# Gated recurrence of a two-block layer on one core: decay sums as pairs of fp32r matmuls, masks one step sooner, three heads' norms together

## What is computed

```python
def gla_scan(k, v, log_a, s0, q):            # 4 heads, dk 128, dv 256, two directions
    # per chunk of 64 positions
    bcum = jnp.cumsum(ac, axis=2)
    b_end = bcum[:, :, -1, :]
    k_to_end = kc * jnp.exp(b_end[:, :, None, :] - bcum)
    s_new = jnp.exp(b_end)[..., None] * s + einsum('bhik,bhiv->bhkv', k_to_end, vc)
    rel = jnp.where(tril, bcum[:, :, :, None, :] - bcum[:, :, None, :, :], -inf)
    scores = einsum('bhjk,bhik,bhjik->bhji', qc, kc, jnp.exp(rel))
    o = einsum('bhji,bhiv->bhjv', scores, vc) + einsum('bhjk,bhkv->bhjv', qc * jnp.exp(bcum), s)

gla_loga = log_sigmoid(dec) / 16             # the decays
y_gla = rmsnorm(gla_o, gla_g_norm) * silu(gla_gate)      # per head, over 256 values
```

## Time and profile before

| | us |
|---|---|
| median of 3 runs | 2233.95 |
| lowest, highest | 2231.99, 2235.13 |
| profiled execution | 2231.3 |
| its span, first to last instruction | 2229.6 |

### The profile page before, as it was taken

One profiled execution on the slowest core, in us unless ns is written; L12 is line 12 of the kernel. 1 busy time (PEld: TensorE's weight loads), 2 busy tenths in 40 slices (PEclk: granted clock), 3 DMA queues, 4 the chain that ended last, 5 costly groups with the idle time before them and its releaser, 6 DMA issues.

```text
span 2229.6 us, 29088 instructions
## 1 busy us (share of the span) xinstructions
PE 2168.6 (97%) x10083; PEld 1742.8 (78%) x10083; DVE 1494.2 (67%) x2235; ACT 1055.2 (47%) x1317; POOL 50.6 (2%) x99
## 2 busy tenths in 40 slices
PE   7999999999999999999999999989999999999998
PEld 6777778878787777877788777768888888888886
DVE  6456657867675888775665677567777777875554
ACT  5344435644444444545433544445555555554443
POOL 0000000000001000000000001000000000000000
PEclk9999999999999999999999999999999999999999
DMA  8877778977777979875444335555655555567664
GB/s 311 280 262 248 270 237 292 325 240 268 243 273 233 316 236 347 305 259 157 132 124 135 104 95 189 173 168 173 199 178 188 180 184 191 179 196 229 193 192 144
DMA packets 279637, 482.03 MB, mean 216 GB/s; under 512 B 21726, under 2 KB 112960, under 8 KB 277744
## 3 DMA queue, kind: packets, MB, share of 16 engines
q1 hardware_dynamic: 274544, 464.93, 63.2%
q0 software_dynamic: 4992, 15.76, 2.1%
HBM read 474.15 MB, written 6.46 MB: 216 GB/s over the span
## 4 chain that ended last, share of the span: by engine, by line
PE 86%; DVE 6%; issue 3%; ACT 3%; DMA 2%; SPq 0%; DVEq 0%; ACTq 0%
PE gemm_ps L1764 74%; DVE w_lo L1035 2%; DMA w_raw<-in_w_in_dram 2%; ACT w_hi L617 1%; PE ps L1808 1%; PE ps L2167 1%; PE ps L2210 1%; DVE tmpT L1067 1%; PE ps L2314 1%; DVE msum L1202 1%; PE ps L2233 1%; DMA w_raw<-in_w_out_dram 1%; PE ps L1847 1%; PE ps L1817 0%; PE ps L1856 0%
## 5 line engine op out<-in xcount | busy, mean ns | idle before, releaser
L1035 DVE TENSOR_TENSOR w_lo<-w_raw,w_hi 128x1024 fp32r<-128x1024 f32 (+1 forms) x688 | 826.9, 1214 | 510.6 <-ACT w_hi L617 504.5
L1764 PE MATMUL gemm_ps<-w_hi,a_hi 128*128 128x512 f32 (+1 forms) x2304 | 920.0, 399 | 26.3 <-DVE w_lo L1035 13.4
L617 ACT ACTIVATE w_hi<-w_raw 128x1024 fp32r<-128x1024 f32 (+1 forms) x688 | 709.7, 1050 | 461.4 <-PE gemm_ps L1764 319.5
L1764 PE MATMUL gemm_ps<-w_hi,a_lo 128*128 128x512 f32 (+1 forms) x2304 | 899.2, 390 | 0.0
L1764 PE MATMUL gemm_ps<-w_lo,a_hi 128*128 128x512 f32 (+1 forms) x2304 | 898.2, 390 | 0.0
L1764 PEld LDWEIGHTS gemm_ps<-w_hi,a_hi 128*128 128x128 f32 x2304 | 435.4, 189 | 144.3 <-issue 29.6
L1764 PEld LDWEIGHTS gemm_ps<-w_hi,a_lo 128*128 128x128 f32 x2304 | 435.1, 189 | 92.7
L1764 PEld LDWEIGHTS gemm_ps<-w_lo,a_hi 128*128 128x128 f32 x2304 | 436.1, 189 | 85.5 <-issue 1.0
L1668 DVE SCALAR_TENSOR_TENSOR acc<-gp,cw,acc 128x256 f32<-128x256 f32 x344 | 151.4, 480 | 13.8 <-DVE acc L1668 1.4
L1202 DVE SCALAR_TENSOR_TENSOR msum<-mraw,cs,msum 128x1024 f32<-128x1024 f32 x120 | 153.0, 1275 | 0.7
L1764 PE MATMUL gemm_ps<-w_hi,ft_hi 128*128 128x512 f32 x344 | 135.0, 392 | 2.2 <-DVE w_lo L1035 2.2
(11 more groups left out here) (402 smaller groups left out, 1448.6 us busy)
## 6 DMA issues: line engine op xcount, KB each, us to landing
w_raw<-in_w_in_dram SPq DMA_DIRECT2D x336, 512.0 KB, 4.6
mraw<-in_w_mod_dram SPq DMA_DIRECT2D x192, 512.0 KB, 6.2
w_raw<-in_w_up_dram SPq DMA_DIRECT2D x336, 256.0 KB, 3.0
w_raw<-in_w_down_dram SPq DMA_DIRECT2D x84, 512.0 KB, 4.3
w_raw<-in_w_out_dram SPq DMA_DIRECT2D x64, 512.0 KB, 4.7
w_raw<-in_w_up_dram SPq DMA_DIRECT2D x24, 512.0 KB, 5.2
x_d<-xres POOLq DMA_DIRECT2D x2, 2048.0 KB, 8.0
x_sb<-in_x_dram SPq DMA_DIRECT2D x2, 1024.0 KB, 5.9
```

Of the source, the lines that this page charges most:

```text
L617: act.activation(w_hi[:, slot, :, 0:n], raw[:, slot, :, 0:n], ACT.Copy).then_inc(hi_done, 1)
L1035: dve.tensor_tensor(w_lo[:, slot, :, 0:n], raw[:, slot, :, 0:n], w_hi[:, slot, :, 0:n].bitcast(F32), ALU.subtract).then_inc(lo_done, 1)
L1764: mm = pe.matmul(gemm_ps[:, bank, rt, 0:n], x[:, chunk0 + k, rt * P:(rt + 1) * P], w[:, slot, kk, 0:n], start=(k == 0 and part == 0), stop ...
```

## The change

It does four things.
1. Each sum of decays, before one float32 matmul, becomes two fp32r matmuls that accumulate in the same bank: one with `la_hi`, the decays' high part, and one with `la_lo`, the rest. ScalarE makes `la_hi` per head (`decays_hi`, at v = 1 of the head before), VectorE makes `la_lo` in place (`decays_lo`, steps 63, 67, 73, 79). `lsum` becomes fp32r: it is loaded raw, without waiting for the state, and ScalarE copies it at step 62; the edge constants are copied in place at step 34. TensorE waits for `la_split` at v = 1.
2. On VectorE `gla_mask` moves from step 65 + k to step 64 + k, and stands behind `gla_mult` of the step.
3. The norms of heads 0 to 2 are taken together at step 91; that of head 3 stays at 96.
4. The buffers `masked` move.

```diff
--- before.py
+++ after.py
@@ -306,7 +306,9 @@
     gates = at("gates", [P, RT, D], F32, 153.5)
     state = at("state", [P, 2, HEADS, GDV], F32, 129.5)
     gqT = at("gqT", [P, 2, 2, T], F32, 137.5)
-    lsum = at("lsum", [P, 2, sum(GROUP_COLS)], F32, 141.5)
+    lsum_raw = at("lsum_raw", [P, 2, sum(GROUP_COLS)], F32, 97.5)
+    lsum = at("lsum", [P, 2, sum(GROUP_COLS)], F32R, 141.5)
+    edge_sums = at("edge_sums", [P, 4 * P], F32R, 80 + CONST_AT["suf_ex"][0] * 4 / KB)
     lexp = at("lexp", [P, 2, LEVELS - 1, 2, HALF], F32, 97.5)
     lq = at("lq", [P, LEVELS - 1, P], F32, 104.5)
     lk = at("lk", [P, LEVELS - 1, P], F32, 108)
@@ -314,7 +316,9 @@
     hsq = at("hsq", [P, RT, GDV], F32, 187.5)
     mden = at("mden", [P, T], F32, 187.5)
     lpair = at("lpair", [P, LEVELS, P], BF16, 149.5)
-    masked = [at("masked0", [P, 4, P], F32, 185.5), at("masked1", [P, 4, P], F32, 201.5)]
+    masked = [at("masked0", [P, 4, P], F32, 93.5), at("masked1", [P, 4, P], F32, 95.5)]
+    la_hi = [at("la_hi0", [P, RT, 2, HD], F32R, 185.5), at("la_hi1", [P, RT, 2, HD], F32R, 201.5)]
+    la_lo = at("la_lo", [P, RT, 2, NBLK], F32R, 189.5)
     sc = at("sc", [P, 4, P], F32, 111.5)
     gtb = at("gtb", [P, D], F32, 129.5)
     gtr = at("gtr", [2, D], F32, 137.5)
@@ -566,8 +570,9 @@
             pool.dma_start(x1_d, xres[:]).then_inc(S("x1_out"), 16)
             sum_store(5, SUMS)
 
+            pool.dma_start(lsum_raw[:], a["lsum"].rearrange("p (d c) -> p d c", d=2)).then_inc(S("lsum_in"), 16)
+            pool.wait_ge(S("lsum_in"), 16)
             pool.wait_ge(S("g_state"), 2)
-            pool.dma_start(lsum[:], a["lsum"].rearrange("p (d c) -> p d c", d=2)).then_inc(S("lsum_in"), 16)
             pool.dma_start(lpair[:], a["lpair"].rearrange("p (l t) -> p l t", l=LEVELS)).then_inc(S("lsum_in"), 16)
             pool.wait_ge(S("y_ready"), 2 * HEADS)
             pool.wait_ge(S("x1_out"), 16)
@@ -841,6 +846,8 @@
                     if m >= 2:
                         act.wait_ge(S("g_kend"), m - 1)
                     act.activation(kexp[m % 2][:, :], (pC, pA)[m % 2], ACT.Exp).then_inc(S("g_kexp"), 1)
+                if s == 34:
+                    act.activation(edge_sums[:, :], C("suf_ex", n=4 * P), ACT.Copy)
                 if 34 <= s < 62:
                     h, i = (s - 34) // 7, (s - 34) % 7 + 2
                     if i == 2:
@@ -856,6 +863,11 @@
                     act.wait_ge(S("g_S"), 1)
                     act.activation(state[:, 0].rearrange("p h v -> p (h v)"), ps[:, 0:2].rearrange("p a b -> p (a b)"),
                                    ACT.Copy).then_inc(S("g_state"), 1)
+                    act.wait_ge(S("g_la"), 8)
+                    act.wait_ge(S("lsum_in"), 16)
+                    for d in range(2):
+                        act.activation(lsum[:, d], lsum_raw[:, d], ACT.Copy)
+                    decays_hi(0)
                 if 64 <= s <= 64 + 6 * HEADS:
                     gla_consume(s - 64)
                 if 66 <= s < 70:
@@ -885,6 +897,12 @@
                 act.wait_ge(S("g_ps"), turn[0] + 1)
                 turn[0] += 1
                 return ps[:, (turn[0] - 1) % 2]
+
+            def decays_hi(h):
+
+                if h:
+                    act.wait_ge(S("la_split"), 2 * h)
+                act.activation(la_hi[h % 2][:], la[:, :, :, h * HD:(h + 1) * HD], ACT.Copy).then_inc(S("la_split"), 1)
 
             def gla_consume(k):
 
@@ -910,6 +928,10 @@
                             act.wait_ge(S("g_mult"), last_use)
                         src = bank[:, 0:GROUP_COLS[g]].rearrange("p (c l s) -> p c l s", c=2, s=HALF)
                         act.activation(lexp[:, :, lo:hi, 1 - d, :], src, ACT.Exp).then_inc(S("g_free"), 1)
+                if v == 1 and h + 1 < HEADS:
+                    if h:
+                        act.wait_ge(S("g_ps"), TURNS(6 * h - 1))
+                    decays_hi(h + 1)
                 if v == 4:
                     for rt in range(RT):
                         bank = take()
@@ -1525,9 +1547,14 @@
                 if s == 62:
                     dve.wait_ge(S("g_S"), 1)
                     dve.tensor_copy(state[:, 1].rearrange("p h v -> p (h v)"), ps[:, 2:4].rearrange("p a b -> p (a b)")).then_inc(S("g_state"), 1)
-                if 65 <= s < 65 + 6 * HEADS + 2:
-                    gla_mask(s - 65)
-                    gla_mult(s - 65)
+                if s == 63:
+                    decays_lo(0)
+                if 67 <= s < 67 + 6 * (HEADS - 1) and (s - 67) % 6 == 0:
+                    decays_lo((s - 67) // 6 + 1)
+                if 64 <= s < 65 + 6 * HEADS + 1:
+                    if s > 64:
+                        gla_mult(s - 65)
+                    gla_mask(s - 64)
                 if s == 72:
                     dve.wait_ge(S("y_ss_m"), HEADS)
                     head_norms(slice(HEADS, 2 * HEADS))
@@ -1535,10 +1562,12 @@
                     if s == 84:
                         dve.wait_ge(evac_act, 40)
                     gated(HEADS + s - 84)
-                if 78 <= s < 78 + 6 * HEADS and (s - 78) % 6 == 0:
-                    h = (s - 78) // 6
-                    dve.wait_ge(S("y_ss"), h + 1)
-                    head_norms(slice(h, h + 1))
+                if s == 91:
+                    dve.wait_ge(S("y_ss"), HEADS - 1)
+                    head_norms(slice(0, HEADS - 1))
+                if s == 96:
+                    dve.wait_ge(S("y_ss"), HEADS)
+                    head_norms(slice(HEADS - 1, HEADS))
                 if s in (92, 93, 98, 99):
                     h = (92, 93, 98, 99).index(s)
                     dve.wait_ge(evac_act, 41 + h // 2)
@@ -1558,6 +1587,11 @@
 
 
             tiles = (((0, 0, T), (1, 0, T), (2, 0, T), (3, P, T)), ((0, 0, T), (1, 0, T), (3, 0, T), (2, 0, P)))
+
+            def decays_lo(h):
+                dve.wait_ge(S("la_split"), 2 * h + 1)
+                own = slice(h * HD, (h + 1) * HD)
+                dve.tensor_tensor(la_lo[:, :, :, own], la[:, :, :, own], la_hi[h % 2][:].bitcast(F32), ALU.subtract).then_inc(S("la_split"), 1)
 
             def gla_mult(k):
 
@@ -2184,7 +2218,11 @@
             def gla_fill(k):
 
                 h, v = k // 6, k % 6
-                L = lambda t, d: la[:, t, d, h * HD:(h + 1) * HD]
+                def sums(out, t, d, of):
+
+                    pe.matmul(out, la_hi[h % 2][:, t, d], of, start=True, stop=False)
+                    return pe.matmul(out, la_lo[:, t, d, h * HD:(h + 1) * HD], of, start=False, stop=True)
+
                 if v == 0 and h < HEADS:
                     if h == 0:
                         pe.wait_ge(S("g_state"), 2)
@@ -2203,19 +2241,18 @@
                     return
                 if v in LEVEL_FILLS:
                     rt, g = LEVEL_FILLS[v]
-                    if k == 1:
-                        pe.wait_ge(S("lsum_in"), 32)
+                    if v == 1:
+                        pe.wait_ge(S("la_split"), 2 * (h + 1))
                     at_col = sum(GROUP_COLS[:g])
                     for d in range(2):
-                        pe.matmul(give()[:, 0:GROUP_COLS[g]], L(rt, d), lsum[:, d, at_col:at_col + GROUP_COLS[g]],
-                                  start=True, stop=True).then_inc(S("g_ps"), 1)
+                        sums(give()[:, 0:GROUP_COLS[g]], rt, d, lsum[:, d, at_col:at_col + GROUP_COLS[g]]).then_inc(S("g_ps"), 1)
                 if v == 4:
                     bank = give()
-                    pe.matmul(bank[:, 0:2 * P], L(0, 0), C("suf_ex", n=2 * P), start=True, stop=True)
-                    pe.matmul(bank[:, 2 * P:3 * P], L(0, 1), C("suf_in"), start=True, stop=True).then_inc(S("g_ps"), 1)
+                    sums(bank[:, 0:2 * P], 0, 0, edge_sums[:, 0:2 * P])
+                    sums(bank[:, 2 * P:3 * P], 0, 1, edge_sums[:, 3 * P:]).then_inc(S("g_ps"), 1)
                     bank = give()
-                    pe.matmul(bank[:, 0:P], L(1, 0), C("pre_in"), start=True, stop=True)
-                    pe.matmul(bank[:, P:3 * P], L(1, 1), C("pre_ex", n=2 * P), start=True, stop=True).then_inc(S("g_ps"), 1)
+                    sums(bank[:, 0:P], 1, 0, edge_sums[:, P:2 * P])
+                    sums(bank[:, P:3 * P], 1, 1, edge_sums[:, 2 * P:]).then_inc(S("g_ps"), 1)
 
             def gla_score(k):
                 if k not in SCORES:
```

## The result

The changed kernel takes 2216.53 us in the median of 4 runs (2212.99 to 2219.43), the kernel before beside it 2232.97 (2231.66 to 2235.13, 4 runs). The ratio is 0.9925, with a 95% interval of 0.9908 to 0.9942: 16.4 us less, where the forecast said 15.0. The profiled execution took 2216.61, with a span of 2214.9, which is 14.7 us under the span before.

What follows compares the result with a forecast made beforehand. TensorE's queue was taken to bound the gated recurrence. Pairs 12.4 + masks 2.6 + norms 0 = 15.0 us off the 2233.95 us median gave 2219.0 us, own range 2215 to 2223, with (a) and most of (b) 2214 to 2227.

Steps and rivals of the forecast that it cites:

- Pairs, 12.4 us: Decay sums in the gated recurrence: two fp32r matmuls each cut four heads from 29.3 to 16.8 us, saving 12.4.
- Masks, 2.6 us: Scores in the recurrence: masks one step sooner remove TensorE's waits of 0.95 and 1.16 us, 2.6 us with longer scores.
- The two terms added up: Whole kernel: savings of pairs and masks simply add, 12.4 + 2.6 + 0 = 15.0 us.
- The rooms: Recurrence: VectorE and ScalarE keep up; 4 us of room behind a mask, products needing 5.1 us against 7.2.
- steps 65 and 81: Tighter places for products, with extra ScalarE work: 6.7 against 7.2 us and 7.5 against 8.2; both still fit.
- the start: First unit after the constants' copies: w_lo ends about 1216.4, TensorE starts at 1216.77; cover 0.4 us, price 0.
- the 4 us behind a mask: VectorE after the sooner mask: 4 us of room before TensorE needs the next unit's split.
- Norms, 0: Joined norms at step 91: 5.2 us less VectorE work, none on the chain, so price 0.
- (a): Rival: saving is larger, unknown prices giving 2.8 us more, part lost to lower clock; about 2214, chance 0.10.
- (b): Rival: thin covers fail or mask waits reach TensorE, say 0.4 us at 16 masks, 6.4 back; 2225.4, chance 0.12.
- (c): Rival: pairs save nothing, two matmuls with two loads costing one fp32; only the waits go; 2231.4, chance 0.04.
- (d): Rival: VectorE waits for scores at the sooner mask, TensorE runs dry, 1.3 us x 16 masks; 2239.8, chance 0.03.

Runs made afterwards that it cites:

- e1: Changed kernel with VectorE's old order (masks at step 65 + k, ahead of products) and norms apart, leaving only the pairs; stage 145.42 us, median 2222.51 us.
- e3: Changed kernel with the four heads' norms taken one by one again; stage 137.38 us, median 2215.24 us.
- e5: Changed kernel with the first multiplication of each mask done two more times on VectorE; stage 141.47 us, 2216.24 us in one run.
- e10: Changed kernel with masks back at step 65 + k, ahead of products, norms still joined; stage 143.16 us, median 2221.27 us.
- e9: Changed kernel with the state's six sums of 512 columns (steps 28 to 31) also made fp32r pairs; stage 137.38 us, median 2215.92 us.

## Why the prediction was right, point by point

- **What bounds the stage.** Right: all 16.26 us came out of TensorE's queue between the two marks, and the rest of the span moved by 1.4 behind them and 0.16 ahead.
- **Pairs, 12.4 us.** Measured behind the masks: 13.3. The sums of a head went from 7.32 to 0.91 + 0.70 + 0.91 + 0.92 + 0.70 = 4.14 us, 12.7 in four heads. The guesses were good: 384 columns 0.175 as assumed, the edge set 0.92 against 0.96, one of its 256-column matmuls 0.17 where 0.12 was taken, its 128-column matmuls 0.06, 0.12, 0.11 and 0.11, 0.10 in the mean where 0.12 was taken. The other 0.6 us is a term that the sum lacked: every unit of the head took 2.77 us before, and after they take 2.73 to 2.77, 2.743 in the mean of six; 24 units x 0.027. Why they are shorter no run here tells. The Trainium skill ("TensorE: Matmul & The Clock Gate", section "LDWEIGHTS (loading the stationary operand)") gives about 0.107 us as the load of 128 columns; the trace comes near it in the mean of the four, 0.10, but the least distance is 0.06. The words of the Trainium skill on what overlaps, which the prediction gives to the section "Measured speedup vs the span model" of that page, stand just ahead of it, under "The mechanism"; 0.227 us between 512-column matmuls with a load each is against them, as 0.231 was.
- **Masks, 2.6 us.** Measured on the kernel before: 2.94, the rest being stops of 0.03 to 0.14 us that only the scores' own times show.
- **The two terms added up.** This step was right only because both edits are in the change. The sum took the waits of the profile before as the whole price of the old order. The pairs alone raise it from 2.9 to 8.0 us, as e1 and e3 show. The plain sum needs that the second edit removes these waits at the new, shorter steps as well; the prediction made sure of that by its rooms, and TensorE's list of waits is empty.
- **The rooms.** The step that failed. The places at steps 65 and 81 and the start (0.4 us of cover, as forecast) held. But the 4 us behind a mask were reckoned from one mask and one split alone; the products and what VectorE does in the same order at some steps only (low part, mLSTM norm, `xn`) were left out. 1.3 us more at each mask already cost 4.1 us (e5), all of it around three places where a late split, the joint norm or `xn` comes on top. A busy VectorE alone is not enough: 92% over 46.40 us cost nothing. It did not harm the forecast, since nothing was added there.
- **Norms, 0.** Right with the new order (e3: 137.38 both), and 2.3 us with the old (e10).
- **Rivals.** (a) is near in size but not in kind: 1.3 us more came out of the stage than forecast, and 1.4 were given back behind it. That the profiled execution came within 0.3 us of its forecast (2216.61 against 2216.3) is therefore luck: pairs and masks were sized 0.9 and 0.3 too small, and a lower clock behind the stage hid it. (b) did not happen: no wait is left. (c) and (d) did not happen.

## What to carry to other kernels

When one engine's work is cut, look at every engine that hands it something in order: places that were barely in time become waits, and the edit that shortens the second engine's path is worth more with the first than alone (8.2 and 2.9 us apart, 16.3 together). Room behind one piece of work has to be counted with everything that the in-order engine does before the next deadline, and at the step where its occasional work falls, since the average head hides that. And an fp32 matmul against constants that fp32r holds exactly could be had for about half its time as two fp32r matmuls (0.45 for 0.86 us at 512 columns, 0.35 for 0.64 at 384; the narrow edge set 0.92 for 1.30), if the copies that it needs lie on an engine that is not on the path there: in the recurrence with the new order they were free, in e9 they cost half of the gain.

## What the runs showed of the hardware

The 1.4 us behind the stage are TensorE's clock and one short stop. The unit behind the next turning took 4.67 us before, from 1485.57, and 5.49 after, from 1469.74. The stretch table over it, before and then after:

```profile
1485.60:1490.20 4.60, 4.60 (x14) 3.62 (x15) 2.56 (x4) 2.94 (x5) 0.00 (x0) 0.61 0.29 83
```

```profile
1469.80:1475.20 5.40, 5.40 (x13) 4.18 (x14) 2.53 (x4) 2.91 (x5) 0.00 (x0) 0.50 0.32 97
```

TensorE had waited about 12 us with a few transposes between in both kernels. Behind it the same twelve matmuls ran with a granted clock of 0.61 in one and of 0.50, the lower of its two levels (1.2 GHz) all the way, in the other: with the transposes behind them 5.11 against 6.18 us. The other 0.36 us lie in the stop itself (11.60 and 11.96 us). Over the traces the same unit took from 4.32 us (e5) to 5.49.

Such spells are what whole times scatter by. One less the mean granted clock, times the length, added up over pieces of 5 us of all that stands behind the stage, gives an estimate of the time lost to the clock there: 9.5 us in e5, 11.9 before, 12.9 after and 14.6 in e9. The same part took 869.96, 872.01, 873.41 and 875.15 us. The four runs of the kernel after say the same: 2212.99 us at a mean granted clock of 0.993, 2216.45 and 2216.61 at 0.991, 2219.43 at 0.990. So only the stage shows an edit of 1 us.

Not expected either: a unit of twelve fp32r matmuls of 512 columns takes 2.73 to 2.77 us in the recurrence after, where nearly all took 2.77 before. It is not what stands ahead of it: the unit at 1274.20 (2.73) has the same fp32 scores ahead as its counterpart before at 1284.08 (2.77). The cause stays open. And a 128-column fp32r matmul can follow its neighbour after 0.06 us in one place although it has a load of its own (0.11 to 0.12 in the other three).
